# The state chain of an RWKV mixer on one core: a chunk's outputs split into three shares, and VectorE's closing operations moved

## The reference, cut to what matters

```python
def step(state, inp):
    r_t, w_t, k_t, v_t, a_t, b_t = inp
    sa = jnp.einsum('bhvk,bhk->bhv', state, a_t)
    state = (state * w_t[:, :, None, :] + sa[..., None] * b_t[:, :, None, :]
             + v_t[..., None] * k_t[:, :, None, :])
    return state, jnp.einsum('bhvk,bhk->bhv', state, r_t)
```

## Time and profile before

| what | us |
|---|---|
| timed runs | 2095.56, 2096.24, 2106.0 |
| profiled execution, its own time | 2107.74 |
| span of the profile, first to last instruction | 2106.0 |
| TensorE busy | 2005.8 (95% of the span) |
| VectorE busy | 655.9 (31%) |
| ScalarE busy | 380.8 (18%) |

### The profile page before, as it was taken

How to read it: one execution, slowest core, us unless ns; L and a number is a source line. 1 busy time by engine, 2 the same in 40 slices (tenths; PEclk the granted TensorE clock), 3 DMA queues, 4 the chain that set the end, 5 groups by cost and what they waited for, 6 DMA issues and landing times. The chain is left out here.

```text
span 2106.0 us, 27777 instructions
## 1 busy us (share of the span) xinstructions
PE 2005.8 (95%) x11658; PEld 1081.6 (51%) x11658; DVE 655.9 (31%) x1323; ACT 380.8 (18%) x731; POOL 68.2 (3%) x131
## 2 busy tenths in 40 slices
PE   8999998899999999998799999989989999999996
PEld 5446984545644444443254488654554444444442
DVE  4245563415411111111044555461343111111112
ACT  3221322414100000000122222151420000000001
POOL 3001000000000000000100010000000000000001
PEclk9999997999999999999999999999989999999998
DMA  8000003201499999999850000022027999999997
GB/s 339 1 1 1 3 3 127 99 21 49 200 379 428 428 428 428 428 427 428 338 227 0 0 2 2 9 120 120 1 120 305 427 428 426 429 427 429 428 428 266
DMA packets 51549, 481.89 MB, mean 229 GB/s; under 512 B 7216, under 2 KB 12080, under 8 KB 23792
## 3 DMA queue, kind: packets, MB, share of 16 engines
q1 hardware_dynamic: 49136, 471.91, 53.6%
q0 software_dynamic: 2304, 8.39, 1.1%
HBM read 461.14 MB, written 19.14 MB: 228 GB/s over the span
## 5 line engine op out<-in xcount | busy, mean ns | idle before, releaser
L2026 PE MATMUL bank<-ring,hT 128*64 128x512 f32 x2080 | 471.2, 595 | 12.0 <-DMA ring<-in_we 8.9
L2026 PEld LDWEIGHTS bank<-ring,hT 128*64 128x64 f32 x2080 | 143.6, 137 | 284.9 <-issue 265.6
L849 PE MATMUL bank<-hT,ring 128*128 128x512 f32 (+1 forms) x608 | 263.3, 593 | 1.8 <-DVE hT L297 1.0
L2019 PE MATMUL bank<-arena 128*128 128x256 f32 x1088 | 252.7, 386 | 0.0
L2033 PE MATMUL bank<-ring,arena 128*64 128x512 f32 x1040 | 237.5, 598 | 10.1 <-DMA ring<-in_we 7.9
L2019 PEld LDWEIGHTS bank<-arena 128*128 128x128 f32 x1088 | 202.5, 191 | 73.8 <-issue 48.7
L849 PEld LDWEIGHTS bank<-hT,ring 128*128 128x128 f32 (+1 forms) x608 | 114.0, 189 | 148.2 <-issue 147.2
L2198 DVE COPY hT<-bank 128x512 f32<-128x512 f32 x68 | 47.0, 691 | 405.6 <-PE bank L2019 405.6
L2178 ACT ACTIVATE arena<-bank 128x256 f32<-128x256 f32 x65 | 24.9, 383 | 672.9 <-PE bank L2005 672.9
L2033 PEld LDWEIGHTS bank<-ring,arena 128*64 128x64 f32 x1040 | 69.0, 136 | 145.5 <-issue 132.7
L1761 PE MATMUL bank<-hT,ring 128*128 128x512 f32 x256 | 110.3, 593 | 2.9 <-PEq L96 2.9
(11 more groups left out here) (434 smaller groups left out, 2040.9 us busy)
## 6 DMA issues: line engine op xcount, KB each, us to landing
ring<-in_we SPq DMA_DIRECT2D x195, 2048.0 KB, 17.7
expert_rows<-arena SPq DMA_DIRECT2D x130, 128.0 KB, 15.0
ring<-in_w_in SPq DMA_DIRECT2D x6, 2048.0 KB, 19.5
ring<-in_w_out SPq DMA_DIRECT2D x4, 2048.0 KB, 10.5
ring<-in_wm SPq DMA_DIRECT2D x2, 2048.0 KB, 17.1
ring<-in_w_in SPq DMA_DIRECT2D x2, 1920.0 KB, 16.8
ring<-in_w_in SPq DMA_DIRECT2D x2, 1664.0 KB, 27.9
ring<-in_w_in SPq DMA_DIRECT2D x2, 1152.0 KB, 30.3
```

What stands on the lines that cost most here:

```text
L849: last = nc.tensor.matmul(B[n % 4][0:w, :], ins_units[unit][:, k, u0:u0 + w], hT[:, k, :], start=k == 0, stop=k == KD - 1)
L2019: last = nc.tensor.matmul(bank[:, o:o + GS], htok[:, i, k * P:(k + 1) * P], selg[z][:, i, :], start=i == 0, stop=i == NT - 1)
L2026: last = nc.tensor.matmul(bank[CAP * j:CAP * j + CAP, :], x[:, k, :], up_w(u, j, k), start=k == 0, stop=k == KD - 1)
```

## The change

Three things are done.

TensorE: `outputs(n)` is split into `out_state(n)`, `out_local(n, 3, V)` and `out_local(n, 2, U)`. The state share now stands directly behind w, ahead of u. kv stands behind u instead of ahead of it. The v share and the U share stand behind st of the same chunk. In the last chunk the v share stands where kv would be. The first matmul alone carries the start flag of the bank. The latents now stand behind all of chunk 1, write bank 6 instead of bank 0, and so wait for ScalarE's copy of chunk 0's outputs.

ScalarE copies the outputs of a chunk directly behind the same chunk's `Um`.

VectorE: the reduction stands between kv and st of chunk 0. The three scalings stand ahead of kv of chunk 1. The reciprocals and the product stand between kv and st of chunk 2.

```diff
-                    def outputs(n):
-
+                    def out_state(n):
                         s, tok = n % 2, slice(n * P, (n + 1) * P)
                         for c in range(RC):
-                            o = slice(c * P, (c + 1) * P)
-                            if n:
-                                nc.tensor.matmul(B[6 + s][:, o], STb[s][:, c, :], rT[:, c, tok], start=True,
-                                                 stop=False)
-                            for m, Z in ((3, fours(Vt[s])), (2, fours(flat(Um)))):
-                                for e in range(2):
-                                    rows = slice(64 * e, 64 * e + 64)
-                                    last = nc.tensor.matmul(B[6 + s][rows, o], Z[:, c, rows],
-                                                            big[s][:, 2 * c + e, m, :], start=n == 0 and m == 3,
-                                                            stop=m == 2)
-                        last.then_inc(s_y, 1)
+                            nc.tensor.matmul(B[6 + s][:, c * P:(c + 1) * P], STb[s][:, c, :], rT[:, c, tok],
+                                             start=c == 0, stop=False)
+
+                    def out_local(n, m, Z):
+                        s = n % 2
+                        for c in range(RC):
+                            for e in range(2):
+                                rows = slice(64 * e, 64 * e + 64)
+                                last = nc.tensor.matmul(B[6 + s][rows, c * P:(c + 1) * P], Z[:, c, rows],
+                                                        big[s][:, 2 * c + e, m, :],
+                                                        start=n == 0 and m == 3 and c == 0,
+                                                        stop=m == 2 and c == RC - 1)
+                        return last
...
-                            if s:
-                                outputs(n - 1)
-                            if n < NT - 1:
-                                for h in range(RH):
...
+                                out_state(n)
...
                             last.then_inc(s_u, 1)
+                            if n < NT - 1:
+                                for h in range(RH):
...
+                                last.then_inc(s_kv, 1)
+                            else:
+                                out_local(n, 3, fours(Vt[s]))
                             eng.wait_ge(s_uc, n + 1)
...
                                 last.then_inc(s_st, 1)
-                            if n == 0:
+                                out_local(n, 3, fours(Vt[s]))
+                            out_local(n, 2, fours(flat(Um))).then_inc(s_y, 1)
+                            if n == 1:
                                 eng.wait_ge(s_l1, 3)
+                                eng.wait_ge(s_yc, 1)
...
-                        outputs(n0 + 1)
...
+                            if n == 0:
+                                eng.wait_ge(s_gq, 1)
+                                eng.tensor_reduce(g_rs, gsq, AX, ALU.add).then_inc(s_gs, 1)
+                            if n == 2:
+                                eng.wait_ge(s_l3, 2)
+                                v(eng.reciprocal(lat, lat))
+                                v(eng.reciprocal(g_rs, g_rs))
+                                f = gv.rearrange("p i (g n) -> p (i g) n", n=RN)
+                                eng.tensor_tensor(f, f, g_rs.unsqueeze(2).to_broadcast([P, 16, RN]), ALU.mult)
                             eng.wait_ge(s_st, n + 1)
                             v(eng.tensor_tensor(Stmp, bu, Stmp, ALU.add))
```

More of the change, by code:

```diff
@@ L963, in _ @@
                             eng.wait_ge(s_stc, 2)
-                            eng.wait_ge(s_lr, 1)
                         for s in range(2):
@@ L971, in _ @@
                                     eng.wait_ge(s_yc, 2)
+                                    eng.wait_ge(s_lr, 1)
                                 for e in range(2):
@@ L1082, in _ @@
                             last.then_inc(s_u, 1)
+                            if n < NT - 1:
+                                for h in range(RH):
+                                    rows = slice(64 * (h % 2), 64 * (h % 2) + 64)
+                                    hs = slice(h * 64, (h + 1) * 64)
+                                    last = nc.tensor.matmul(B[5][rows, (h // 2) * 64:(h // 2) * 64 + 64],
+                                                            Kt[s][:, hs], Vt[s][:, hs], start=True, stop=True)
+                                last.then_inc(s_kv, 1)
+                            else:
+                                out_local(n, 3, fours(Vt[s]))
                             eng.wait_ge(s_uc, n + 1)
@@ L1090, in _ @@
                                 last.then_inc(s_st, 1)
-                            if n == 0:
+                                out_local(n, 3, fours(Vt[s]))
+                            out_local(n, 2, fours(flat(Um))).then_inc(s_y, 1)
+                            if n == 1:
                                 eng.wait_ge(s_l1, 3)
+                                eng.wait_ge(s_yc, 1)
                                 for i in range(NT):
                                     t, rows = slice(i * P, (i + 1) * P), slice(32 * i, 32 * i + 32)
-                                    nc.tensor.matmul(B[0][rows, 0:P], lat_pick[:, 0, :], sq14[:, t], start=True,
+                                    nc.tensor.matmul(B[6][rows, 0:P], lat_pick[:, 0, :], sq14[:, t], start=True,
                                                      stop=False)
-                                    nc.tensor.matmul(B[0][rows, 0:P], lat_pick[0:96, 1, :], sq15[0:96, t], start=False,
+                                    nc.tensor.matmul(B[6][rows, 0:P], lat_pick[0:96, 1, :], sq15[0:96, t], start=False,
                                                      stop=False)
-                                    last = nc.tensor.matmul(B[0][rows, 0:P], lat_pick[:, 2, :], sqkv[:, t],
+                                    last = nc.tensor.matmul(B[6][rows, 0:P], lat_pick[:, 2, :], sqkv[:, t],
                                                             start=False, stop=True)
                                 last.then_inc(s_l2, 1)
-                        outputs(n0 + 1)
                 @block.gpsimd
@@ L1169, in _ @@
                             eng.activation(flat(Um), B[2][:, :], ACT.Copy).then_inc(s_uc, 1)
[L1170 to L1176, removed]
+                            eng.wait_ge(s_y, n + 1)
+                            eng.activation(rT[:, :, n * P:(n + 1) * P], fours(B[6 + s][:, :]), ACT.Copy).then_inc(s_yc, 1)
                 @block.vector
@@ L1249, in _ @@
                                 eng.tensor_tensor(flat(Wm[s]), B[4][:, :], flat(Wm[s]), ALU.add).then_inc(s_wc, 1)
+                            if n == 1:
+                                eng.wait_ge(s_l1, 3)
+                                eng.tensor_scalar(t14, t14, col("cq_g", 0), None, ALU.mult)
+                                eng.tensor_scalar(cq2[0:96, :], cq2[0:96, :], col("cq_g", 1)[0:96, :], None, ALU.mult)
+                                eng.tensor_scalar(ckv, ckv, col("ckv_g"), None, ALU.mult)
                             if n == NT - 1:
@@ L1270, in _ @@
                             eng.wait_ge(s_l2, 1)
[L1271 to L1281, removed]
+                            eng.tensor_copy(lat_rows, B[6][:, 0:P]).then_inc(s_lr, 1)
                     k1, k2 = kr[:, :, 0:HALF], kr[:, :, HALF:2 * HALF]
```

## The result

Six timed runs of the changed kernel gave a median of 2083.19 us (2078.68 to 2085.47), beside 2099.25 us for the kernel before (six runs, 2095.56 to 2106.0). The ratio is 0.9896, with a 95% interval of 0.9866 to 0.9927. The forecast was 2082 us. A second set of runs gave 2082.8 against 2106.62 us, ratio 0.9888 (0.9860 to 0.9917). The profiled execution of the changed kernel took 2081.6 us with a span of 2079.9 us, 26.1 us less than the profiled span before.

The account below looks back on a forecast made before the run. TensorE, busy 95% of the span, and its chain were taken as the bound. From 2096.24 us, 13.0 for two layers' chains and 1.3 once or twice for the clock gave 2080.6 to 2081.9; forecast 2082, 8-in-10 range 2075 to 2090.

Parts of the forecast that it names:

- u of chunk 0 to w of chunk 1: Pair 1: VectorE's reduction holds the state block by 0.9 us, so w starts at 248.2 instead of 247.93, a 0.3 us loss.
- w to u of chunk 1: Pair 1: only the state share stands between w and u, 3.42 us falls to 2.0, a gain of 1.4 us.
- u to the products: Pair 1: from u of chunk 1 to the next pair's products, 7.32 us falls to 6.66, a gain of 0.7 us.
- w of chunk 2 to w of chunk 3: Pair 2: formerly 6.88 us; reciprocals and product hold st's addition by 1.4 us, a loss of 1.4 us.
- From there to the next block: Pair 2: from w of chunk 3 to the next block, 12.8 us at full clock falls to 6.7, a gain of 6.1 us.
- The bound without any hold: Both layers: if VectorE's moved operations held nothing, the sum would be 2 x 2.3 = 4.6 us lower.
- no fall would be left in the chain: Pair 2: the clock stays up, saving 8.5, 2.7 and 1.3 us against the profiled execution.
- The clock's share: Timed kernel before: only 1.3 us, once or twice, was taken from the 2096.24 us median for the clock.
- A fall in pair 2: Rival: the clock still falls in pair 2, 7 us a layer, 2089 us with one layer, 2096 with both; chance 0.13.
- A fall in pair 1: Rival: the clock falls at the 0.9 us pause in chunk 0, 11.2 us a layer, up to 2118 us; chance 0.04.
- The outputs were no burden: Rival: u of chunks 1 and 3 waited for something else, only 1.3 us of clock gained, 2095 us; chance 0.04.
- The bound with slow shares: Split output shares take 1.5 us each, not 0.85, costing 5 us in all, 2087 us; 0.02 deducted from faster.

Follow-up runs that it names:

- e3: Kernel before, with only VectorE's six closing operations where the changed kernel has them: 2103.95 us against 2106.62, ratio 0.9989.
- e1: Changed kernel with VectorE's reduction (chunk 0) and reciprocals and product (chunk 2) ahead of its wait for kv: 2076.44 us, ratio 0.9868 to the kernel before.
- e2: Changed kernel's TensorE and ScalarE lists, with VectorE's closing operations where the kernel before has them: 2079.1 us, ratio 0.9877 to the kernel before.
- e6: e1 with the latents' twelve matmuls moved behind the products of chunk 2's third quarter: 2078.82 us, ratio 0.9889 to the kernel before.
- e8: Changed kernel with v and U shares mixed by quarter behind st, state share still behind w: 2084.11 us, ratio 0.9893 to the kernel before.
- e5: Kernel before, with three idle 128x512 matmuls in TensorE's pause ahead of w of chunk 3: 2097.52 us against 2106.05, ratio 0.9970.
- e7: Kernel before, with three idle 128x256 matmuls in TensorE's pause ahead of w of chunk 3: 2093.76 us against 2106.03, ratio 0.9949.
- e4: Changed kernel with the three output shares put together again, whole and behind st: 2099.43 us, ratio 0.9979 to the kernel before.

## Why the prediction was right

**The steps.** Each in layer 0, predicted and measured. u of chunk 0 to w of chunk 1: 5.9 and 5.70 us. w to u of chunk 1: 2.0 and 1.97. u to the products: 6.66 and 6.58. w of chunk 2 to w of chunk 3: 8.25 and 8.18. From there to the next block: 6.7 and 6.76. The lists give 2.08 - 1.30 + 5.86 = 6.64 us a layer, the last term against 12.62 us at full clock (e3), where 6.5 were predicted. Two layers are 13.3 us.

**VectorE's part.** The prediction held that reduction and product would hold the state block, since kv had left its place ahead of u. TensorE's pauses are there, 0.58 and 1.12 us, both released by VectorE, where 0.9 and 1.3 were predicted. TensorE is done with the shares 5.12 us after u begins, where the sum had 4.96, and in pair 1 w begins 5.70 us after u, where it had 5.86. e1 and e2 show the loss, and e3 with e2 that it comes from the two moves together and from neither alone. The bound without any hold was 2.3 us lower a layer; e1 is 1.8 lower.

**The clock.** Predicted was that no fall would be left in the chain. All profiles of the changed kernel, of e1, e2, e6 and e8 agree, and e5 and e7 show the cause: with the lists of before and the pause filled, no fall in any of four chains, while with the pause open (the kernel before and e3) it fell in three of four. In the profiled executions the falls cost 8.7 + 2.7 + 1.5 = 12.9 us (21.30 and 14.13 less 12.62, and 7.83 less 5.12), and 13.3 + 12.9 is 26.2 of the 26.1 us between the spans. That this comes out so close is luck. The two chains themselves are 15.33 and 8.17 us shorter, 23.5 in all. Between the end of the first and the start of the second the two kernels take the same, 943.69 and 943.94 us, so that the 2.7 us at the start of the next block are lost again before layer 1's chain. Behind the second chain the changed kernel takes 3.3 us less, and ahead of the first 0.4 us more, with the same instructions in both.

**What was mis-sized.** The clock's share in a typical run of the kernel before. The prediction took 1.3 us once or twice, from three timed runs with a median of 2096.24 us. In 57 more timed runs (the three sets of the table, 17, 23 and 17) the kernel before lay between 2094.63 and 2120.49 us with medians of 2106, and e7 is 12 us below that. The changed kernel stayed at 2083, for it no longer has the falls; so its forecast held while the gain over the kernel before grew from the predicted 14 us to 16 and then 24. The term to correct is the one of the base, not of the change. That the forecast came within 1.2 us owes something to the base of 2096.24 us, near the fastest runs of the kernel before, which goes with a small term for the clock. From the later medians of 2106 the same terms would have given 2092.

**The rivals.** A fall in pair 2 was not seen in any profile with the shares split. A fall in pair 1 was seen, but in e4 only, in one of its two layers, and it lasted some 7 us and cost 2.8 us, not 11.2. "The outputs were no burden" is refuted by w to u of chunk 1, 3.42 to 1.97 us, and by the first stretch, 16.33 to 14.25 us. The bound with slow shares did not come either: a share took 0.88 and 0.97 us, where 0.85 and 1.5 were weighed.

Open: what decides whether the clock falls behind a pause that allows it, and where the dips of the clock outside the chains come from. They are in all profiles, they shift the whole time by some us from one profile to the next, and no run took them apart.

## What to carry to other kernels

When an operation is moved into a wait, redraw the wait with all moves of the same change in place: VectorE's wait between kv and st was 3.18 us long in the old list and is 0.40 us in the new one (e1), and the long one has gone to the other side of kv (2.72 us). Here it paid to cut the outputs where the tile shape changes, and to put each share behind work of its own shape. And count pauses as clock: the pause of 1.57 us, once in each layer, cost its own length and, by the medians, some 12 us more a program, which 1.3 us of idle matmuls in each gave back.

## What the hardware showed that was not expected

The clock fell behind two pauses of 0.59 and 0.84 us (e4, layer 1) and not behind the same two in layer 0. It fell behind 0.69 and 1.57 us in both layers of the kernel before, and behind 0.69 and 1.50 us in layer 0 of e3 and not in layer 1. It didn't fall behind a single 1.12 us (six chains). Once down it stayed down for some 7 us in one case (e4, layer 1), for under 4 us in another (layer 1 before) and for over 26 us in a third (layer 0 before), with TensorE busy in most of it:

```profile
306.70:333.50 26.80, 25.08 (x111) 17.34 (x112) 6.31 (x17) 2.94 (x5) 1.80 (x2) 0.50 0.05 15
1337.40:1340.40 3.00, 3.00 (x21) 2.16 (x19) 2.81 (x7) 0.00 (x0) 0.00 (x0) 0.50 0.00 0
```

Matmuls of two tile shapes in turns took longer than the same matmuls sorted by shape. One quarter of whole outputs, 2 rows of 128x128 and 8 of 128x64, takes 1.01 us (e4, e3), while the same instructions sorted by shape take 0.24 + 0.46 us; in four quarters the difference is 1.2 us.
